# Alternating the high and the low products of the weight-stationary matmuls in an fp32 two-block transformer kernel

## What is computed

```python
def memory_cross_attn(x, mem_k, mem_v, wq, wo):
    q = (x @ wq).reshape(B, S, XATTN_HEADS, XATTN_HD)     # 1024 x 1024, two layers
    ...
def sq_relu_mlp(x, w1, b1, w2, b2):
    return jnp.square(jax.nn.relu(x @ w1 + b1)) @ w2 + b2  # x @ w1: 1024 x 4096, two layers
def swiglu(h, w_gate, w_up, w_down):
    return (jax.nn.silu(h @ w_gate) * (h @ w_up)) @ w_down # gate and up: 1024 x 2816
```

## Time and profile before

| | |
|---|---|
| median of 3 runs | 953.45 us (952.93 to 953.58) |
| span of the profiled execution | 1903.2 us |
| PE busy in it | 1896.1 us, 5108 matmuls |
| PEld busy | 1373.0 us, 5108 loads |
| DVE, ACT, POOL busy | 710.1, 520.2, 60.6 us |
| HBM read | 201.09 MB |

### The profile page before, as it was taken

One profiled execution on the slowest core, in us unless ns is written; L12 is line 12 of the kernel. 1 busy time (PEld: TensorE's weight loads), 2 busy tenths in 40 slices (PEclk: granted clock), 3 DMA queues, 4 the chain that ended last, 5 costly groups with the idle time before them and its releaser, 6 DMA issues.

```text
span 1903.2 us, 13114 instructions
## 1 busy us (share of the span) xinstructions
PE 1896.1 (100%) x5108; PEld 1373.0 (72%) x5108; DVE 710.1 (37%) x963; ACT 520.2 (27%) x732; POOL 60.6 (3%) x96
## 2 busy tenths in 40 slices
PE   9999999999999999999999999999999999999998
PEld 9669766766777776767666777667887667777766
DVE  6323234425343332443343343334334442232232
ACT  4233221313222223122132222232233232222221
POOL 0000000000000001000000000001000000000010
DMA  7332142215434433032154344341310243223200
GB/s 261 132 103 74 66 143 89 74 59 176 146 133 137 150 133 111 1 145 76 50 174 151 133 144 137 129 147 50 111 67 22 89 136 96 89 89 110 89 22 22
DMA packets 109660, 203.00 MB, mean 107 GB/s; under 512 B 4332, under 2 KB 75264, under 8 KB 106272
## 3 DMA queue, kind: packets, MB, share of 16 engines
q1 hardware_dynamic: 106000, 189.15, 29.7%
q0 software_dynamic: 3168, 12.24, 1.8%
q10 hardware_dynamic: 432, 0.79, 0.1%
HBM read 201.09 MB, written 1.06 MB: 106 GB/s over the span
## 4 chain that ended last, share of the span: by engine, by line
PE 99%; issue 0%; ACT 0%; DVE 0%; POOLq 0%; POOL 0%; ACTq 0%
PE WB L377 20%; PE YB L402 12%; PE YB L395 12%; PE YB L410 12%; PE WB L380 10%; PE YB L463 6%; PE WB L395 3%; PE WB L410 3%; PE WB L402 3%; PE WB L359 2%; PE WB L366 2%; PE WB L362 2%; PE YB L879 2%; PE WB L745 2%; PE WB L501 1%; PE YB L852 1%
## 5 line engine op out<-in xcount | busy, mean ns | idle before, releaser
L1801 DVE TENSOR_TENSOR wl<-raw,wh 128x2048 fp32r<-128x2048 f32 x144 | 331.5, 2306 | 283.4 <-ACT wh L1161 279.5
L377 PE MATMUL WB<-XS,wh 128*128 128x512 f32 x832 | 410.8, 675 | 0.0
L377 PEld LDWEIGHTS WB<-XS,wh 128*128 128x128 f32 x832 | 245.3, 303 | 118.0 <-issue 107.4
L1161 ACT CAST wh<-raw 128x2048 fp32r<-128x2048 f32 (+1 forms) x147 | 278.6, 1898 | 156.7 <-PE YB L410 84.3
L380 PEld LDWEIGHTS WB<-XS,wl 128*128 128x128 f32 x832 | 211.3, 317 | 35.3 <-issue 32.4
L380 PE MATMUL WB<-XS,wl 128*128 128x256 f32 x832 | 215.9, 440 | 0.0
L402 PE MATMUL YB<-wl,FHT 128*128 128x512 f32 x344 | 196.5, 676 | 0.0
L410 PE MATMUL YB<-wh,FLT 128*128 128x512 f32 x344 | 196.3, 674 | 0.0
L395 PE MATMUL YB<-wh,FHT 128*128 128x512 f32 x344 | 196.2, 673 | 0.0
L1343 ACT COPY U<-WB 128x256 f32<-128x256 f32 x102 | 33.0, 375 | 411.9 <-PE WB L380 411.9
L410 PEld LDWEIGHTS YB<-wh,FLT 128*128 128x128 f32 x344 | 103.1, 300 | 57.5 <-issue 49.5
(11 more groups left out here) (373 smaller groups left out, 1803.2 us busy)
## 6 DMA issues: line engine op xcount, KB each, us to landing
raw<-in_mlp_w SPq DMA_DIRECT2D x64, 1024.0 KB, 5.2
raw<-in_w_ada_t SPq DMA_DIRECT2D x24, 1024.0 KB, 4.8
raw<-in_mlstm_w_in SPq DMA_DIRECT2D x11, 1024.0 KB, 5.3
raw<-in_w_ffn_down SPq DMA_DIRECT2D x11, 1024.0 KB, 4.8
raw<-in_w_ffn_gate SPq DMA_DIRECT2D x10, 1024.0 KB, 5.4
raw<-in_w_ffn_up SPq DMA_DIRECT2D x10, 1024.0 KB, 5.3
raw<-in_mem_w_kv SPq DMA_DIRECT2D x8, 1024.0 KB, 5.1
raw<-in_xattn_wq SPq DMA_DIRECT2D x8, 1024.0 KB, 5.1
```

Of the source, the lines that this page charges most:

```text
L377: e.matmul(W[:, :], H[:, at(k)], XS[:, k, :], start=k == 0, stop=False)
L1161: f = e.copy(w[:, 0:a * b], raw[:, 0:a * b])
L1801: f = e.tensor_tensor(L[:, 0:a * b], raw[:, 0:a * b], H[:, 0:a * b].bitcast(F32), ALU.subtract)
```

## The change

In each block the two loops over k become one. After the first high product comes the wait for the low part, then the first low product, then the second high product, and so on. The accumulation into the bank is the same sum in another order.

```diff
                     e.wait_ge(*w_hi[m])
                     for k in range(8):
                         e.matmul(W[:, :], H[:, at(k)], XS[:, k, :], start=k == 0, stop=False)
-                    e.wait_ge(*w_lo[m])
-                    for k in range(8):
+                        if k == 0:
+                            e.wait_ge(*w_lo[m])
                         p = e.matmul(W[:, 0:256], L[:, at(k)], XH[:, k, :], start=False, stop=k == 7)
```

## The result

The changed kernel takes 957.52 us (957.36 to 957.74, four runs) against 953.52 us before: a ratio of 1.0041, 95% interval 1.0029 to 1.0053. It is 4.0 us slower, just above the upper end of the range (957.5) and on the side that had 0.15.

A forecast was written before the change was run, and what follows sets the result against it. TensorE's stream of matmuls was taken as the bound, its work halved in a timed run; alternating (0) plus the earlier wait (0) left 953.4 us, range 950.5 to 957.5 us.

The forecast's parts named there:

- What bounds the kernel: Whole kernel: TensorE's stream of matmuls from first to last, busy 1896.1 of 1903.2 us in the profile.
- the total halves: All TensorE work is halved in a timed run: half the profiled span is 951.6 us, the median 1.9 us above.
- Part one: In the 104 blocks of L377 and L380, alternating high and low products costs nothing at the seams; taken as 0.
- The sign that was to show a right prediction: Load track's idle time should move from L377 to L380 without changing the sum.
- Part two: The wait for low weights moves ahead by seven 512-column products, 1.6 us timed; slack holds everywhere; taken as 0, bound 8.2 us.
- The tightest place: Last feed-forward's wide block after a normalization: low weights at 11.5 us, needed at 12.4, slack 0.9 us.
- The first rival: Slower: the earlier low-weight wait binds at five blocks after normalizations, up to 961.7 us; chance 0.12.
- The second rival: Faster: loads not hidden behind 256 columns at full pace and running further ahead than one; 941.6 us, chance 0.12.
- an unforeseen cost of alternating as such: Slower case at the alternating products, no size given; chance 0.03.
- The range's upper end: Whole kernel: 957.5 us, set at half of the bound of the moved low-weight wait.

The follow-up runs named there:

- new profile of before: The kernel before, unedited, profiled again, this time at the full pace of the timed runs; 953.79 us, ratio 0.9998.
- the half loads: Changed kernel with seven of eight products per block loading 64 of 128 weight columns: low products' loads 954.19 us, high products' 948.12 us, one run each.
- twos: Against the kernel before: two high products, then two low ones, four times per block, the low wait after the first two highs; 953.06 us, ratio 0.9993.
- fours: Against the kernel before: four high products, then four low ones, twice per block; 955.40 us against 953.55, ratio 1.0019.
- The interleaved run: Against the kernel before: a chunk's two halves interleaved into two PSUM banks, sixteen high products in turn, then sixteen low; 961.42 us, ratio 1.0080.

## Why the prediction was wrong

**What bounds the kernel** was right: TensorE fills the span at full pace too (942.1 of 951.8 us in the new profile of before), though not quite without waits: the chain that ended last is TensorE for 83% of that span, where it was 99%. That the total halves was right, but in part by luck: a block is 2787 ns and not half of 5.61 us, some 2 us less in all, and TensorE is idle for 9.7 us, where half of its idle time in the earlier trace rows would be 3.6. That everything on TensorE is the same thing halved was not right. In the earlier trace rows a row of lows goes at 236 ns and a row of highs at 465, as their columns. At full pace it is 120 against 227, where 113.5 would be in proportion. The shortest loads do not keep the proportion: 199 ns on the record at the halved pace, 187 after the change. The mean ones come nearer to it, 317 ns against 190 in the new profile of before, so the record does not tell how long a load really occupies TensorE.

**Part one, the step that failed**: "a product costs the longer of its own stream and the load of the next one", and from it that the order cannot matter. Two things in it were wrong. The border times 0.44 and 0.22 us, read from the earlier trace rows, were to halve, to 220 and 110 ns, and cost nothing on top; after the change they are 236 and 117 ns, where the settled products of the new profile of before take 227 and 120. And the sum does depend on the order: the same sixteen streams and sixteen loads take 2787 ns in rows and 2824 ns one by one. A load that is not done when its stream ends is on the record still running in the next stream; that it lengthens that stream is argued from the half loads.

In rows of eight the lows pay 6 ns each, and of the highs behind them only the first five (26 ns in sum, of which the first two lows give some 8 back); one by one every high product pays some 9 ns and every low one gives back 3. Against 8 x 340.7 = 2726 ns, what the streams take with half loads of the high weights, a block loses 61 ns in eights and 98 ns one by one, 6.3 us and 10.2 us over the 104 blocks. The term of the sum was 0 and measured 3.8 us of the 4.0.

The sentence that "if a load were not quite hidden behind 256 columns at the full pace, it would stay so after the change" named the weak point and decided it wrongly; the 317 ns of the earlier trace rows against a stream of 236 ns had been put down to queueing. The sign that was to show a right prediction, idle time of the load track moving from L377 to L380, went the other way: 28.9 to 38.0 us at L377, 8.1 to 1.6 us at L380. A load behind a long stream is done about 0.05 us before that stream, and this gap stands ahead of the next load, that of L377.

**Part two was right.** The tightest place came out as worked out. From the timeline of after at the feed-forward's first wide block:

```profile
773.08 4.49 DVE L1801 TENSOR_TENSOR wl<-raw,wh 128x2048 fp32r<-128x2048 f32 x2
...
776.12 0.39 PE L377 MATMUL WB<-XS,wh 128*128 128x512 f32 x1
776.34 0.28 PE L380 MATMUL WB<-XS,wl 128*128 128x256 f32 x1
```

The low part is there at 773.08 + 2.25 = 775.33 and L380 starts at 776.34: 1.0 us of slack where 0.9 was predicted. At the attention's first block it is 2.0 us where 2.1 was predicted. The first rival did not come true, and moving the wait alone cost nothing.

**The second rival** had half of its premise right and the conclusion wrong. Loads are indeed not hidden behind 256 columns at full pace, but they do not run further ahead than one: no load of these products, in any trace here, starts before the matmul ahead of it has started (2 ns after it at the earliest). Alternating then makes the exposed load dearer, not cheaper. The Trainium skill ("TensorE: Matmul & The Clock Gate", the section on LDWEIGHTS) gives a load as columns/1.2, 107 ns here by estimate, which I took as hidden behind 118 ns (half of 236). The traces do not bear that out: rows of low products take 120 ns with full loads, and the half load of the high weights brings the short stream to 113.7 ns. The window that pulls loads ahead of running matmuls, on the same page of the Trainium skill (the architectural detail on queue depths), shows in no run as more than one load ahead.

**Chances and range.** What happened is the case that got 0.03, "an unforeseen cost of alternating as such". The range's upper end came from a rival that had no part in it.

**What stays open**: why the long products need five to settle after short ones, why twos cost nothing against eights while fours do, and what the load and the stream share. The half loads, in one run each, show that the loss goes when the loads behind the short streams are halved with their products' outputs, and shrinks when those behind the long ones are; they do not show the mechanism. With 64 columns the load's record (134 ns) is longer than its 114 ns stream by 20 ns, and yet nothing is lost; behind 384 columns it is longer by 13 ns only (188 against 175), and the long product still takes 232 ns. So the record alone is not the measure.

## What to carry to other kernels

Do not judge an order of matmuls from a profile at another pace than the timed runs: compare span and time first, and if they differ, profile again before working anything out. Where the next weight load does not fit behind a short stream, what it costs depended here on what follows: of the orders within one bank, short and long products one by one were the worst, and rows and twos were equal. Look for the distance between starts, not for the mean duration or a wait: this loss has no idle time and no releaser.

## What the runs showed of the hardware that was not expected

The profile of before lasted twice as long as the timed runs at a granted clock of 1.000. I had read that as the lower of the two levels of TensorE's clock. The interleaved run has a spell at that level (granted clock 0.50), and there 512 columns take 427 ns, not the 445 ns of the earlier trace rows; so that level alone does not account for the pace of the first profile. Its page also lacks the row of the granted clock over time that every other page has, so its 1.000 may be no reading at all; what slowed that execution stays open. With full loads, products that differ from their neighbours in width cost 10 ns a pair over their own streams even with 384 against 512 columns (407 against 227 + 170, the latter an estimate by proportion from 227), and equal widths cost nothing.
